# Converting weight chunks whole instead of in halves, and six subtractions moved from GpSimd to VectorE

## What is computed

```python
for l in range(DEPTH):
    if l % 2 == 0:   # gated short convolution + top-k sparse attention, one projection
        z = _rmsnorm(x, p["g_mix"][l]) @ p["w_in_even"][e]
        ...
        x = x + jnp.concatenate([y_a, y_b], axis=-1) @ p["w_out_even"][e]
    else:            # gated linear recurrence
        z = _rmsnorm(x, p["g_mix"][l]) @ p["w_in_odd"][o]
        ...
        x = x + (jax.nn.gelu(gate) * y_c) @ p["w_out_odd"][o]
    x = x + _mem_attn(_rmsnorm(x, p["g_x"][l]), mem_k[l], mem_v[l], ...)
    ...
    x = x + (jax.nn.gelu(g) * val) @ p["w_down"][l]
```

## Time and profile before

| what | value |
|---|---|
| median of 3 runs | 1722.95 us (1720.61 to 1725.6) |
| the profiled execution, its own time | 1725.6 us |
| its span, first to last instruction | 1723.1 us |
| mean granted TensorE clock | 0.971 of full speed |
| TensorE matmul busy | 1646.0 us (96%) |
| VectorE busy | 999.8 us (58%) |
| ScalarE busy | 636.8 us (37%) |
| GpSimd busy | 635.2 us (37%) |

### The profile page before, as it was taken

The page is one execution under the profiler, slowest core; times in us unless marked ns, Lnnn a source line. Parts: engine busy times, 40 slices in busy tenths (PEclk is TensorE's granted clock), DMA queues, the critical chain, the costliest instruction groups (busy, mean ns, idle before and its releaser), DMA issues.

```text
span 1723.1 us, 31013 instructions
## 1 busy us (share of the span) xinstructions
PE 1646.0 (96%) x11890; PEld 1549.2 (90%) x11890; DVE 999.8 (58%) x1316; ACT 636.8 (37%) x975; POOL 635.2 (37%) x307
## 2 busy tenths in 40 slices
PE   5999988899899999999999979999899999999999
PEld 5959863799599999999999979799689999999999
DVE  5668997455555556455555779555635555035530
ACT  4332246333434333133323655433524333123320
POOL 2315460133033333333334645633123334333332
PEclk9969998899999999999999989999989999999999
DMA  4322340124022222222222322424012222222232
GB/s 170 112 86 98 114 134 2 34 81 167 13 98 74 85 85 101 70 86 85 95 92 86 105 89 75 134 87 172 25 39 80 90 85 92 86 78 85 85 101 87
DMA packets 41713, 153.48 MB, mean 89 GB/s; under 512 B 5344, under 2 KB 5856, under 8 KB 40360
## 3 DMA queue, kind: packets, MB, share of 16 engines
q1 hardware_dynamic: 41640, 152.46, 26.2%
HBM read 145.22 MB, written 9.32 MB: 90 GB/s over the span
## 4 chain that ended last, share of the span: by engine, by line
PE 75%; issue 11%; POOL 5%; DVE 4%; ACT 3%; DMA 1%; POOLq 0%; DVEq 0%; SPq 0%; ACTq 0%
PE PS L818 67%; POOL WLO L405 5%; PE AX L1073 2%; DVE RB L1539 1%; PE AX L1010 1%; PE AX L982 1%; PE PS L993 1%; PE AX L876 1%; PE AX L1079 1%; ACT WHI L447 1%; ACT LG L614 0%; PE PS L1045 0%; DVE RSTD L1188 0%; DVE SQA L1206 0%; PE AX L1042 0%
## 5 line engine op out<-in xcount | busy, mean ns | idle before, releaser
L405 POOL TENSOR_TENSOR WLO<-WRAW,WHI 128x1024 fp32r<-128x1024 f32 (+3 forms) x299 | 634.7, 2132 | 1070.1 <-ACT WHI L447 1070.0
L447 ACT ACTIVATE WHI<-WRAW 128x1024 fp32r<-128x1024 f32 (+3 forms) x299 | 268.8, 919 | 740.0 <-PE PS L818 680.8
L818 PE MATMUL PS<-XH,WHI 128*128 128x274 f32 x2256 | 478.0, 293 | 23.3 <-POOL WLO L405 16.5
L818 PE MATMUL PS<-XH,WLO 128*128 128x274 f32 x2256 | 475.0, 292 | 0.0
L818 PE MATMUL PS<-XL,WHI 128*128 128x274 f32 x2256 | 472.8, 291 | 0.0
L818 PEld LDWEIGHTS PS<-XH,WHI 128*128 128x128 f32 x2256 | 361.3, 190 | 27.5 <-POOL WLO L405 18.5
L818 PEld LDWEIGHTS PS<-XL,WHI 128*128 128x128 f32 x2256 | 360.5, 191 | 0.0
L818 PEld LDWEIGHTS PS<-XH,WLO 128*128 128x128 f32 x2256 | 359.8, 191 | 0.0
L818 PE MATMUL PS<-HH,WHI 128*128 128x274 f32 x1216 | 256.6, 292 | 0.7 <-DVE HL L1393 0.7
L818 PE MATMUL PS<-HH,WLO 128*128 128x274 f32 x1216 | 254.1, 290 | 0.0
L818 PE MATMUL PS<-HL,WHI 128*128 128x274 f32 x1216 | 253.9, 290 | 0.0
(11 more groups left out here) (232 smaller groups left out, 1639.2 us busy)
## 6 DMA issues: line engine op xcount, KB each, us to landing
WRAW<-in_w_in_even SPq DMA_DIRECT2D x29, 512.0 KB, 3.6
WRAW<-in_w_up0a SPq DMA_DIRECT2D x22, 512.0 KB, 3.6
WRAW<-in_w_up0b SPq DMA_DIRECT2D x22, 512.0 KB, 3.6
WRAW<-in_w_up1a SPq DMA_DIRECT2D x22, 512.0 KB, 3.6
WRAW<-in_w_up1b SPq DMA_DIRECT2D x22, 512.0 KB, 3.6
WRAW<-in_w_mv SPq DMA_DIRECT2D x16, 512.0 KB, 3.6
WRAW<-in_w_xq SPq DMA_DIRECT2D x16, 512.0 KB, 3.5
WRAW<-in_w_xo SPq DMA_DIRECT2D x16, 512.0 KB, 3.7
```

What stands on the lines that cost most here:

```text
L405: pool.tensor_tensor(WLO[parity][:, first:last], WRAW[parity][:, first:last], WHIf[parity][:, first:last], ALU.subtract).then_inc(lo_done, ...
L447: act.activation(WHI[parity][:, first:last], WRAW[parity][:, first:last], ACT.Copy).then_inc(hi_done, 2 // len(cuts))
L818: ins = pe.matmul(dst, w, x, start=first, stop=last)
```

## The change

Three things change together. First, no chunk is converted in halves: ScalarE and GpSimd do each chunk in one instruction, the counters count one for each chunk, and TensorE waits for a whole chunk. Second, the subtractions of chunks 2 to 7 of `mv0` are done by VectorE, one ahead of each of its six steps. Third, GpSimd passes over these six, waits for the last of them, and then goes on with `out_even`.

```diff
-IN_HALVES = {*range(C0["in_even"] + EVEN_HEAD, C0["mv0"] + 8), *range(C0["odd"], C0["out_odd"] + 2)}
-
-
-def parts(c, cols, halved=False):
-
-    return [(1, 0, 512), (2, 512, cols)] if halved or c in IN_HALVES else [(2, 0, cols)]
+DVE_LO = range(C0["mv0"] + 2, C0["mv0"] + 8)
...
             def load(c, src, cols, parity):
                 if not isinstance(c, int) or c >= 2:
-                    sp.wait_ge(lo_done, c * 2 - 2)
+                    sp.wait_ge(lo_done, c - 1)
...
+            def lo(c, cols, parity):
+
+                pool.wait_ge(hi_done, c + 1)
+                pool.tensor_tensor(WLO[parity][:, 0:cols], WRAW[parity][:, 0:cols], WHIf[parity][:, 0:cols],
+                                   ALU.subtract).then_inc(lo_done, 1)
...
-                if c == C0["out_even"]:
-
-                    pool.wait_ge(chunk_done, c)
+                if c == DVE_LO.start:
+
+                    c = DVE_LO.stop
+                    pool.wait_ge(lo_done, c)
+                    pool.wait_ge(chunk_done, C0["out_even"])
                     unused_columns(A_TILES, KT)
...
+                act.activation(WHI[parity][:, 0:cols], WRAW[parity][:, 0:cols], ACT.Copy).then_inc(hi_done, 1)
...
-                pe.wait_ge(lo_done, c * 2 + (1 if halved else 2))
+                pe.wait_ge(lo_done, c + 1)
...
-                    if halved and k == kt // 2:
-                        pe.wait_ge(lo_done, c * 2 + 2)
...
+                        pe.wait_ge(lo_done, c + 1)
                         for kk in range(2):
                             k = 2 * q + kk
-                            pe.wait_ge(lo_done, c * 2 + kk + 1)
...
-            for step in range(6):
+            for c in DVE_LO:
+                dve.wait_ge(hi_done, c + 1)
+                dve.wait_ge(lo_done, c)
+                dve.tensor_tensor(WLO[c % 2][:, 0:1024], WRAW[c % 2][:, 0:1024], WHIf[c % 2][:, 0:1024],
+                                  ALU.subtract).then_inc(lo_done, 1)
+                step = c - DVE_LO.start
```

More of the change, by code:

```diff
@@ L415, in _ @@
             while c < N_CHUNKS:
-                if c == C0["out_even"]:
-                    pool.wait_ge(chunk_done, c)
+                if c == DVE_LO.start:
+                    c = DVE_LO.stop
+                    pool.wait_ge(lo_done, c)
+                    pool.wait_ge(chunk_done, C0["out_even"])
                     unused_columns(A_TILES, KT)
-                halved = c in IN_HALVES
-                stop = min(x for x in (C0["out_even"], C0["odd"], C0["mv1"], N_CHUNKS) if x > c)
+                stop = min(x for x in (DVE_LO.start, C0["odd"], C0["mv1"], N_CHUNKS) if x > c)
                 pair, n = COLS[c:c + 2], 0
-                while c + 2 * n + 2 <= stop and COLS[c + 2 * n:c + 2 * n + 2] == pair and all(
-                        (c + 2 * n + k in IN_HALVES) == halved for k in range(2)):
+                while c + 2 * n + 2 <= stop and COLS[c + 2 * n:c + 2 * n + 2] == pair:
                     n += 1
                 if n == 0:
-                    lo(c, COLS[c], c % 2, halved)
+                    lo(c, COLS[c], c % 2)
                     c += 1
@@ L432, in _ @@
                     for k in range(2):
-                        lo(i * 2 + (c + k), pair[k], (c + k) % 2, halved)
+                        lo(i * 2 + (c + k), pair[k], (c + k) % 2)
                 c += 2 * n
@@ L821, in chunk @@
             def chunk(c, parity, t, slot, kt, rh, rl, ready=None, base=0, skip=0, halfway=None, behind=None):
-                halved = isinstance(c, int) and c in IN_HALVES
-                pe.wait_ge(lo_done, c * 2 + (1 if halved else 2))
+                pe.wait_ge(lo_done, c + 1)
                 if not isinstance(t, int) or t >= 2:
```

## The result

The changed kernel takes 1738.11 us (median of four runs, 1736.64 to 1744.08), against 1723.8 us for the kernel before beside it. The ratio is 1.0092, with a 95% interval from 1.0062 to 1.012: slower, by 14.3 us between the medians and 15.9 by the ratio. The forecast was 1732.8 us and +0.57%; the measured time lies inside the range of 1725 to 1741, near its top, and just outside the likeliest case's own 1728 to 1738. The profiled execution took 1742.67 us, with a span of 1740.9.

What follows compares the result with a forecast made beforehand. TensorE was busy 96%, but turns and `mv0` were taken as bound by both engines, from the second turn rather by VectorE. 2.2 + 0 + 3.1 + 3.5 + 1.0 = 9.8 us gave a median of 1732.8 us, range 1725 to 1741.

Steps and rivals of the forecast that it cites:

- likeliest case: Whole kernel: the forecast's own case, slower, 1728 to 1738 us, given a chance of 0.62.
- the clock's rival: Turns, odd layer, `mv0`, attention, `mv1`: new waits lower TensorE's clock, up to 7.5 us more, 1740 us; chance 0.13.
- The price on TensorE: Behind key chunks: whole conversion usable after 3.65 us, TensorE waits about 1.1 us each, seven followers 7.7 us.
- The turns' term: Four turns: VectorE sets the pace and hides most TensorE delays; end 2.2 us late, bounds 1.0 and 4.0.
- The port's term: Turns, port shared by VectorE and GpSimd: three two-input instructions end about the same time; zero, bounds -1.5 and +1.5.
- the upper bound just given: Shared port: a longer GpSimd instruction could block VectorE for its full 2.4 us, called the upper bound.
- `mv0` was right: `mv0`: six subtractions of 1.23 us join VectorE's queue; last eviction +4.5 us, net +3.1, bounds 0 and +6.
- The attention's -1.4: Attention: ScalarE's table load ends 1.7 us behind the last eviction in place of 3.1, giving 1.4 us back.
- Odd layer and `mv1`: Odd layer +3.5 us from key chunks' followers, bounds 1 and 6; `mv1` and `out_odd` +1.0, bounds 0 and 3.
- The signs named: New trace: followers 3.6 to 4.2 us after ScalarE, GpSimd waits +5 to 8, attention +5 to 8, `out_odd` +8 to 12.
- Absorption: Turns and `mv0`: VectorE's pace swallows TensorE's delays and the move pays for itself; +3 us, 1726.0 us, chance 0.18.
- less blocking: Shared port: whole subtractions block VectorE less than two pieces; 6.5 us faster, 1716.5 us, chance 0.07.

Runs made afterwards that it cites:

- e6: Kernel before without the turns' 41 `topk` rounds (tiny memsets instead) and with whole chunks in turns and `mv0`; one execution, turns 8.1 us longer than in e5.
- e5: Kernel before, halves kept, with the 41 rounds of `topk` in the four turns replaced by tiny memsets; one execution, turns 93.3 us against 99.5.
- e1: Kernel before with every chunk converted whole and GpSimd keeping all subtractions of `mv0`; 1737.6 us, ratio 1.0098.
- e4: Kernel before with whole chunks in the turns and `mv0` only, halves kept in the odd layer, `mv1` and `out_odd`; 1731.95 us, ratio 1.0061.
- e3: Kernel before with ScalarE converting whole chunks and TensorE waiting for all of each, GpSimd still subtracting in two pieces; 1732.43 us, ratio 1.0059.
- e8: Kernel before with the subtractions of chunks 2 to 7 of `mv1`, not `mv0`, done by VectorE; 1721.5 us, ratio 0.9987.
- e9: Kernel before, halves kept, VectorE subtracting chunks 2 to 7 of `mv0`, whose seven `topk` rounds move into the attention; 1731.23 us, ratio 1.0051.
- e7: Kernel before with GpSimd subtracting each half in two pieces, ScalarE and TensorE as before; 1719.24 us, ratio 0.9975.

## Why the prediction was right, and where it was off

The forecast had the sign, the order of size and most of the stages, and the total lies in its range. But the turns, where the largest part of the loss lies, were forecast at less than a third of what they measured. That alone is 5.1 us, and the total stayed inside only because the range had been drawn wide, up to 1741 us, for another reason (the clock's rival): that part is luck.

**The price on TensorE was right.** 3.65 us from ScalarE's start to a usable chunk was forecast, 3.58 measured, and seven followers at 1.1 make 7.7 against 8.1 in e6 less e5.

**What hides it was wrong, and this is the step that failed.** The turns' term was 2.2 us, with bounds of 1 and 4, because "I take TensorE to have the further delays in hand" after the second turn. It measured 7.3, and 6.1 to 6.9 in e1 and e4 with the same code there. The windows of the turns, before and changed, then e1 and e3, have the columns of the earlier trace rows:

```profile
122.80:222.30 99.50, 95.60 (x729) 95.10 (x728) 91.68 (x183) 25.09 (x46) 52.04 (x38) 0.96 0.32 106
```

```profile
124.00:230.80 106.80, 98.15 (x728) 96.65 (x727) 99.48 (x184) 23.38 (x27) 47.18 (x19) 0.95 0.30 100
```

```profile
123.50:229.10 105.60, 97.29 (x729) 95.76 (x728) 95.49 (x184) 23.39 (x27) 48.34 (x19) 0.95 0.31 100
```

```profile
123.20:228.20 105.00, 95.61 (x729) 94.07 (x728) 93.60 (x184) 23.39 (x27) 52.19 (x38) 0.97 0.31 101
```

Length less matmul time is TensorE's waiting: 3.9 us before, 8.65 changed, 8.3 in e1, 9.4 in e3. So 4.8 of the 7.3 us are new waits, and 2.5 are the same matmuls taking longer, by an estimate 1.4 for the lower granted clock (5% of 106.8 us in place of 4% of 99.5) and the rest for the overlap lost at each wait. The forecast let TensorE's delays vanish in the time for which it waits for VectorE anyway. But that time was short: by e5, VectorE holds TensorE back by only 6.2 us over the four turns, with waits in the third and the fourth turn alone. And TensorE's waits for VectorE hardly shrank, since VectorE itself got later: 3.9 us before, 3.4 in e1, 3.5 in e3, and 5.7 in the changed kernel. In e1 and e3 it waited for TensorE at four and five evictions, 5.9 and 7.2 us. In the changed kernel it waited only once, 3.0 us, but was held up inside its instructions: 99.5 us busy in place of 91.7, with the same work.

**The port's term** was zero, bounds -1.5 and +1.5, since three instructions in a row end at the same time either way. For VectorE that was wrong. The convolution's last instruction takes 2.80 in place of 1.70 us, and the CB and YC products lose 0.67 and 0.46 each: 4 x (1.10 + 0.67 + 0.46) = 8.9 us, of which 3.0 come back in the instruction ahead. For the end of the turns, by which the term was counted, it nearly held. e1 and the change lie 0.6 and 1.8 us above e3 there, but 0.7 and 1.0 of that is the first key chunk, which runs partly at half clock in all of them and took 3.8 us in e3, 4.5 in e1 and 4.8 in the changed kernel. Since e3 also waits 1.0 us more for GpSimd than e1, the port's share of the turns is 0 to 2 us, and these runs can't say it closer. Where the port did cost is the odd layer: whole subtractions are 3.6 and 4.7 us slower there than pieces (e1 and the change against e3). The remark that 2.4 us "is the upper bound just given" is a slip: the bound given was +1.5.

**`mv0` was right**, for the change as a whole: +4.5 forecast, +5.2 measured, or +5.8 against e8. The subtraction took 1.22 us where 1.23 was worked out. VectorE's busy time in the stage grew by 2.9 us for 7.3 us of subtractions, so 4.4 us of contention were given back, against 4.2. e9 takes 3.9 of the 5.4 us away by clearing the queue. The attention's -1.4 can't be told in its length, which moves by 3.5 us from trace to trace, but its mechanism shows: ScalarE's table load ends 1.55 us behind the last eviction in the changed kernel, 3.1 before (2.5 in e8), and 1.7 was forecast.

**Odd layer and `mv1`** were +3.5 and +1.0, and measured +2.7 and +1.8. The followers of key chunks did what was forecast. By the timeline of the matmuls three of them keep TensorE waiting for 0.9, 1.0 and 1.2 us, 3.2 in all, where before it had one wait of 0.5. Behind them, where the forecast let further lateness fall into the 7.6 us wait, TensorE's waits change from 1.2 us for GpSimd and 7.6 for VectorE to 4.8 and 2.1. The table of waits of the changed kernel, 925 to 1130 us:

```profile
PE PS L808 <- POOL WLO L398: 8.1, 5, 4.8
...
PE PS L808 <- DVE MK L1289: 2.1, 1, 2.1
```

The 4.8 us are not GpSimd's own. It had been idle for 8.4 us until ScalarE converted the chunk at 1031.0 us, behind its gate functions and a table load, and these had waited for a convolution instruction of VectorE (L1533) that took 3.49 us. With pieces on the port (e3) these last waits are 3.1 us in all in place of 6.9, while the followers wait 3.7: this is what the port costs here, and the sum had no term for it.

**Not in the sum:** the 1.2 us up to the turns. About a third is seen already at chunk 9, which also had halves and had been counted free, and behind it TensorE waits 0.9 us in the indexer where it waited 0.2; how much of this is noise is open, for the stage took 122.0 to 122.8 us in the traces that keep the halves and 122.4 to 124.0 in those that don't. The clock's rival did not come true where it was placed: `mv0` kept a granted clock of 1.00, and the two cross-attentions cancel within 0.4 us. Only the 1.4 us in the turns are of its kind.

**The signs named.** The followers start 3.58 us after ScalarE, at the edge of the 3.6 to 4.2 named, and the six subtractions take 1.2 us. TensorE's wait for GpSimd in the turns grew by 2.9 us, not 5 to 8 (4.9 in e1, 6.6 in e6): in the changed kernel part of the delay turned into waits for VectorE. The attention's first matmul comes 13.3 us later, not 5 to 8, and `out_odd` begins 19.5 us later in the traces, not 8 to 12; the profiled execution lies 4.6 us above its median, the one before 2.65.

**The rivals.** Absorption was the error of the forecast itself, in part, and less blocking was its opposite: shorter pieces, not longer ones, free VectorE (e7). (Its sum also comes to 6.1 rather than 6.5 us, and 56 chunks stay with GpSimd, not 52.) What stays open: how the loss of the turns divides between the two engines in the changed kernel itself, since each experiment that frees one lets the other lead, and whether the move costs anything on top of whole chunks.

## What to carry to other kernels

Where two engines share a port, try the helper's work in shorter pieces: here two more cuts gave 0.25%, though they made GpSimd's total work grow. Taking the halves away cost 1.0%, a third of it by the port (5.2 of 15.5 us, e1 against e3); the rest stays when only TensorE's early start is taken away. Before calling an engine that never rests the bound, compare its instructions' lengths with what they take alone, and ask by how much it holds the others back: here VectorE was busy 92 of 99.5 us and held TensorE back by 6.2 (e5), too little to hide 8.1 us of delays that begin in the first turn. Move work to an engine by where it is free, stage by stage: the same six subtractions on VectorE cost 5 us beside `topk` and gained 2 us in `mv1`.

## What the runs showed of the hardware

How long VectorE is held up follows the length of the neighbour's single instruction more than its total: in the turns 1.70 us for one convolution instruction beside pieces of 1.28 us, 2.80 beside wholes of 2.4, and in the odd layer a mean of 1.44 falling to 1.10 when the pieces were cut once more. It works both ways: a whole subtraction of GpSimd took 4.89 us in place of 2.4 (e1, `mv1`). Even a copy of 128x2 elements took up to 2.16 us beside whole subtractions, as this row of the changed kernel's timeline of VectorE shows (start, length, instruction), beside a subtraction from 162.61 to 164.99; its neighbour L1327, of the same form, took 0.16:

```profile
162.86 2.16 DVE L1326 COPY AST<-UB 128x2 f32<-128x2 f32 x1
```

Stretches of half TensorE clock fall differently in each trace: the same cross-attention took 104.3 or 105.8 us, with a granted clock of 0.97 or 0.95, and the same attention 64.8 or 68.2, with 0.88 or 0.81.
